# Squared-relu layers: four of the eight scaled copies of x on POOL, the first relu-and-square sooner, the norm's sums one product later

## The reference, cut to what matters

```python
D_FF_2 = 4 * D_MODEL

def sq_relu_mlp(h, w1, w2):
    u = jax.nn.relu(h @ w1)
    return (u * u) @ w2
# in the second block, for l in 0, 1:
#   x = x + mixer(rmsnorm_2(x, norm_mix))
#   x = x + sq_relu_mlp(rmsnorm_2(x, norm_mlp[l]), w1[l], w2[l])
```

## Time and profile before

| | |
|---|---|
| median of 3 runs | 2420.86 us (2419.38 to 2427.39) |
| profiled execution, its own time | 2424.04 us |
| its span | 2422.2 us |
| TensorE busy | 2370.7 us, 98% of the span |
| VectorE, ScalarE, GpSimd busy | 1328.1, 1065.5 and 232.8 us |
| mean granted TensorE clock | 0.994 of full speed |
| chain that ended last | PE 84%, DVE 6%, ACT 5%, issue 3%, DMA 2% |
| the two squared-relu MLPs | from about 1472 and 2058 us of the span |

### The profile page before, as it was taken

The page is one execution under the profiler, slowest core; times in us unless marked ns, Lnnn a source line. Parts: engine busy times, 40 slices in busy tenths (PEclk is TensorE's granted clock), DMA queues, the critical chain, the costliest instruction groups (busy, mean ns, idle before and its releaser), DMA issues.

```text
span 2422.2 us, 30917 instructions
## 1 busy us (share of the span) xinstructions
PE 2370.7 (98%) x12252; PEld 1948.2 (80%) x12252; DVE 1328.1 (55%) x2135; ACT 1065.5 (44%) x1759; POOL 232.8 (10%) x189
## 2 busy tenths in 40 slices
PE   9999999999999999999999999999999899999998
PEld 8888888777777788888887667989987677888987
DVE  5533436688654345433435866735645675763653
ACT  4323224455432334322223456624624785741642
POOL 0100100322102010100100300000000100100100
PEclk9999999999999999999999999999999999999999
DMA  4223223211122132323222214536521112644642
GB/s 153 100 86 104 99 84 105 80 53 53 62 70 72 55 118 70 105 86 114 88 86 88 82 49 131 141 112 157 140 96 61 42 47 64 165 122 120 160 121 70
DMA packets 72865, 230.68 MB, mean 95 GB/s; under 512 B 8081, under 2 KB 16529, under 8 KB 72465
## 3 DMA queue, kind: packets, MB, share of 16 engines
q1 hardware_dynamic: 66096, 205.81, 25.8%
q0 software_dynamic: 6048, 22.02, 5.5%
q10 hardware_dynamic: 576, 0.87, 0.1%
HBM read 226.57 MB, written 2.10 MB: 94 GB/s over the span
## 4 chain that ended last, share of the span: by engine, by line
PE 84%; DVE 6%; ACT 5%; issue 3%; DMA 2%; POOL 0%; POOLq 0%; ACTq 0%; DVEq 0%
PE bank L2158 21%; PE bank L2162 21%; PE bank L2160 21%; PE bank L2176 3%; PE bank L2178 3%; PE bank L2180 3%; PE bank L2342 2%; ACT whi L2463 2%; DMA wraw<-in_stream 2%; PE bank L2304 1%; PE bank L2349 1%; PE bank L2249 1%; PE bank L2245 1%; DVE wlo L2811 1%; PE bank L2247 1%
## 5 line engine op out<-in xcount | busy, mean ns | idle before, releaser
L2811 DVE TENSOR_TENSOR wlo<-wraw,whi 128x1024 fp32r<-128x1024 f32 (+3 forms) x462 | 518.2, 1126 | 556.4 <-ACT whi L2463 555.7
L2463 ACT ACTIVATE whi<-wraw 128x1024 fp32r<-128x1024 f32 (+3 forms) x462 | 435.4, 949 | 469.4 <-PE bank L2162 375.5
L2158 PE MATMUL bank<-hhi,whi 128*128 128x512 f32 x1288 | 514.9, 400 | 2.3 <-ACT hhi L2508 1.0
L2162 PE MATMUL bank<-hhi,wlo 128*128 128x512 f32 x1288 | 504.8, 392 | 1.7 <-DVE wlo L2811 1.6
L2160 PE MATMUL bank<-hlo,whi 128*128 128x512 f32 x1288 | 503.8, 391 | 0.4 <-DVE hlo L2862 0.4
L2158 PEld LDWEIGHTS bank<-hhi,whi 128*128 128x128 f32 x1288 | 242.3, 188 | 57.1 <-issue 7.1
L2162 PEld LDWEIGHTS bank<-hhi,wlo 128*128 128x128 f32 x1288 | 242.1, 188 | 56.0 <-DVE wlo L2811 4.4
L2160 PEld LDWEIGHTS bank<-hlo,whi 128*128 128x128 f32 x1288 | 242.5, 188 | 50.2 <-DVE hlo L2862 2.7
L2160 PE MATMUL bank<-mlo,whi 128*128 128x512 f32 x448 | 176.8, 395 | 0.2 <-DVE mlo L3168 0.2
L2158 PE MATMUL bank<-mhi,whi 128*128 128x512 f32 x448 | 176.9, 395 | 0.0
L2162 PE MATMUL bank<-mhi,wlo 128*128 128x512 f32 x448 | 176.9, 395 | 0.0
(11 more groups left out here) (459 smaller groups left out, 4232.9 us busy)
## 6 DMA issues: line engine op xcount, KB each, us to landing
wraw<-in_stream SPq DMA_DIRECT2D x335, 512.0 KB, 3.5
wraw<-in_stream POOLq DMA_DIRECT2D x34, 512.0 KB, 5.9
wraw<-in_stream SPq DMA_DIRECT2D x32, 192.0 KB, 2.4
wraw<-in_stream SPq DMA_DIRECT2D x22, 256.0 KB, 2.7
rot_tables<-in_stream SPq DMA_DIRECT2D x8, 512.0 KB, 5.2
rot_tables<-in_stream POOLq DMA_DIRECT2D x8, 512.0 KB, 5.4
wraw<-in_stream SPq DMA_DIRECT2D x26, 128.0 KB, 2.0
wraw<-in_stream SPq DMA_DIRECT2D x8, 320.0 KB, 2.9
```

Of the source, the lines that this page charges most:

```text
L2158: pe.matmul(out, sh, xh, start=first, stop=False)
L2162: p = pe.matmul(out, sl, xh, start=False, stop=end and last)
L2463: act.activation(whi[j][:, 0:L], src[:, 0:L], F.Copy).then_inc(*hi.up(c))
L2811: dve.tensor_tensor(wlo[j][:, 0:L], src[:, 0:L], whi[j][:, 0:L].bitcast(f32), SUB).then_inc(*lo.up(c))
```

## The change

Three edits, the same in both MLPs. The scaled copies for feature tiles 0 to 3 go from ACT (an activation with a scale) to POOL (a multiplication by the gain); those for tiles 4 to 7 stay on ACT, and DVE's combination now waits for both. The relu, square and split of plain tile 0 goes ahead of `token_sums(2)`, and `token_sums(3)` goes behind that of plain tile 1. A job that does nothing (`int`) is put between the seven additions and the two `R.step`, so that each of these comes one product later.

```diff
                 ts[0] = run(ts[0])
                 one_more_split()
                 token_sums(1)
+                square(ts[0], 0, afree)
+                one_more_split()
                 token_sums(2)
-                one_more_split()
-                token_sums(3)
                 state["held"] = False
-                square(ts[0], 0, afree)
                 for f in range(1, 4):
                     state["held"] = f == 3
                     square(run(ts[f]), f, afree)
-                owed = chain_of([open_sums[R.next].pay_one] * 7, [R.step] * 2)
+                    if f == 1:
+                        token_sums(3)
+                owed = chain_of([open_sums[R.next].pay_one] * 7, [int], [R.step] * 2)
...
-                elif k == "plain":
+                elif k == "plain" and a[1] >= 4:
                     s, j, q, after = a
                     waits(after)
                     act.activation(tmps[:, q, :], X(s)[:, j, :], F.Copy, scale=gain(s, j)).then_inc(*held.up(("plain", s, j)))
...
                     u1, u2, v1, v2 = tmps[:, u, 0:256], tmps[:, u, 256:512], tmps[:, v, 0:256], tmps[:, v, 256:512]
+                    w.wait_ge(*gated["plain", s, k4])
                     w.wait_ge(*held["plain", s, k4 + 4])
...
+                elif k == "plain" and a[1] < 4:
+                    s, j, q, after = a
+                    waits(after)
+                    w.wait_ge(*before.now())
+                    pool.tensor_scalar(tmps[:, q, :], X(s)[:, j, :], gain(s, j), None, MUL).then_inc(*gated.up(("plain", s, j)))
+                    before = gated
                 elif k == "acc":
                     kind, key, r, plus, settled = a
                     w.wait_ge(*(landed(r) if kind == "low" else added[key] if kind == "row" else lo[settled]))
```

## The result

| | before | after |
|---|---|---|
| median, 6 runs each on the same chip | 2420.72 us (2419.38 to 2427.39) | 2439.04 us (2436.76 to 2443.31) |
| profiled execution, its own time | 2424.04 us | 2438.38 us |
| its span | 2422.2 us | 2436.5 us |
| granted clock | 0.994 | 0.99 |

The ratio on record is 1.007, with a 95% interval of 1.0059 to 1.008; between the two medians lie 18.3 us. The changed kernel is slower. The forecast was 15.7 us slower and 2436.6 us, in a range of 2430.0 to 2442.5 us.

The account below looks back on a forecast made before the run. TensorE, busy 98% of the span, was taken to bound the kernel, so its waits count. 7.76 + 8.21 - 0.3 = 15.7 us on 2420.86 gave 2436.6 us, range 2430 to 2442.5 us.

Parts of the forecast that it names:

- The decisive step: POOL's first copy in each MLP can't begin before its first accumulating DMA is through, at 1487.04 in the first.
- The first sum: DVE's first token sum waits for POOL's first copy, taken as 0.70 us: 8.30 and 8.75 us later.
- TensorE's idle at the third tile: First MLP: TensorE idle from 1484.65 to 1490.83 for `whi3`, third matmul at 1492.1: 7.0 us lost.
- ACT's chain: First sum to the second seven-product chunk's `whi`: 17.6 us, 0.54 less than before; 7.76 and 8.21 us lost per MLP.
- The step from TensorE's 7.0 us to ACT's longer delay: At the third product TensorE waits for ACT again, so the first MLP loses ACT's 7.76 us, not 7.0.
- The norm: Sums one product later: their wait goes, one of 1.63 us at the second MLP's spread comes; together -0.3 us.
- the one on the root: Second MLP's norm: DVE's root stands behind an `mlo` awaiting the `mhi` of 2134.04, beginning at 2135.30 instead of 2132.59.
- The clock: A 1.2 GHz stretch follows the long idle in both MLPs, hidden in lost time: counted nothing, at most 2.5 us each.
- The first, copies in time: Copies run in time and ACT is relieved; head waits of 2.5 and 2 us go: 2416 us, 5%.
- The second, part taken back: ACT's chain isn't the later one, so only TensorE's own loss counts, 4.5 us per MLP: 2430 us, 10%.
- The third, an unhidden low clock: Slow clock outlasts the slack or comes before the seven products, up to 2.5 us per MLP: 2437 to 2442 us, 18%.
- The fourth: The first MLP's slow stretch at the norm goes with the sums' wait and no other comes: 2434 us, 7%.

Follow-up runs that it names:

- the kernel with one copy: The changed kernel with the copies of tiles 1 to 3 back on ACT, only each MLP's first on POOL: 2439.27 us, ratio 1.0065.
- copies alone: The changed kernel with the old order of relus and token sums and without the `int`; POOL's copies stay: 2439.89 us, ratio 1.0074.
- the gap alone: The kernel before with only the norm's sums one product later and its spread two products behind them: 2416.56 us, ratio 0.9979.

## Why the prediction was right, and where its terms were off

**The decisive step held.** The copies stand behind the DMA's wait, the landing is hardly moved by the change, and the copies begin with the wait's end. From the issue at 1478.79 on SP to POOL's DMA at 1484.45 are 5.66 us, and before it was 1480.37 to 1486.03, the same 5.66 us. With the DMA elsewhere the loss is gone, and with the DMA one copy later it is a third.

**The first sum: 8.30 and 8.75 us were forecast, 9.2 us came in both.** Counted from the `wlo` ahead of it, the sum began 1.22 us after that before and 10.44 us after it in after, 9.22 us later (second MLP: 1.23 and 10.38, 9.15 us). The term that was mis-sized is POOL's copy. I took 0.70 us between bounds of 0.53 and 1.29; it took 1.86 us behind the DMA, 1.95 us next, and 1.56 us in the other two places. It is outside my upper bound, too: I had reasoned that one input can't cost more than two. The bound was the fastest of the groups that I could have read. The trace of before has other POOL instructions of 128x512 with two inputs at a mean of 1454 ns (a multiplication, too), 1505 and 1534 ns (sums); with the slowest of them the bound would have been near the 1.56 us of an undisturbed copy:

```profile
L3355 POOL TENSOR_TENSOR qk<-ftmps 128x512 f32<-128x512 f32 x28 | 43.0, 1534 | 2.2
```

The copy's 1.16 us more are partly made up by its beginning 0.78 us after the DMA's start and not 1.01, and, in the second MLP, by a landing that comes 0.5 us sooner after the `wlo` (7.84 us, where it was 8.35). The estimate from the Trainium skill's "GPSIMD Engine Reference", "Elementwise — side-by-side cycle accounting", 0.44 us, was farther off still. By it the sum would have been 0.5 us less (0.26 us twice) and not the 0.3 us that the prediction says.

**TensorE's idle at the third tile:** about 6 us for `whi3` and then its `wlo` were forecast; 7.28 and 6.13 us came, and 0.32 us for the `wlo`. Two labels of the prediction are off without touching a sum: the first MLP has a fifth short wait before the change, 0.53 us for a `wlo` at 1479.55 in the second tile, and it is still there in after; and the waits that I said would remain "at the second and third product" are both the third's.

**ACT's chain: 17.6 us were forecast, 18.44 us came** (1487.13 to 1505.57; before 18.14). My list of gaps came from rows in which POOL was quiet. With POOL copying, three of them are longer: sum to `thi` 1.60 us for 1.19, `whi3` to `wlo` 1.37 us for 1.08, and `wlo` to the third sum 1.53 us for 1.22. That is 1.0 us; the other gaps come to 0.17 us less than my list. So the lighter ACT gave back nothing, where I had put 0.54 us per MLP. Even with the copies in time it is little: in the kernel with the DMA behind them the same chain takes 17.80 us (1482.33 to 1500.13), 0.34 us less than before. That this is POOL beside DVE and not the order is shown by the kernel with one copy, where the same gaps are 1.19, 1.07 and 1.28 us. The step from TensorE's 7.0 us to ACT's longer delay held, as did its sign: at the third product TensorE was late by 9.5 and 9.4 us (7.76 and 8.21 forecast). In the first MLP that is 9.22 + 0.30, the late sum and the chain's 0.30 us over before.

**The norm: -0.3 us were forecast, -2.1 us came** in the kernel with that edit alone. The wait at `ident` was 1.53 and 1.01 us and not 1.63. The step that failed is the one on the root. I had it behind an `mlo` that waits for the `mhi` of 2134.04. But the `mlo` just ahead of the root takes an earlier `mhi`. ACT's and DVE's timelines of after, first MLP, show it: the `mlo` begins before ACT's next `mhi` does.

```profile
1557.01 0.64 ACT L2498 ACTIVATE mhi<-tmps 128x512 fp32r<-128x512 f32 x1
...
1556.77 0.68 DVE L2858 TENSOR_TENSOR mlo<-tmps,mhi 128x512 fp32r<-128x512 f32 x1
1557.37 0.15 DVE L2878 TENSOR_SCALAR sm<-bank 128x4 f32<-128x4 f32 x1
```

The shorter waits are worth some 0.7 us in the two MLPs together (0.1 and 0.6). The rest may be the slow stretch of clock behind the sums ("What the runs showed of the hardware"), which is not shown by medians: the interval is wide enough to hold the forecast's 0.3 us and those 0.7 us alone.

**The clock.** A granted clock of 0.50, which is 1.2 GHz, did follow the long idle in both MLPs, and the matmuls behind it took 0.80 us. It was hidden as argued: TensorE still waited 0.93 and 0.89 us for ACT's `whi` at the third product.

**The rivals.** The first, copies in time, fell with the idle of 9.21 us. Its price was wrong as well: the kernel in which the copies are in time takes 2417.91 us and the norm's edit alone 2418.87, so what the timely copies and the new order add to that edit is within the scatter. The 2.5 and 2 us at the heads went only in small part: the first MLP still has three waits of some 0.8 us in that kernel, 2.44 us in all (the third is 0.76 us, for the `wlo` at 1507.54), and the second has 1.46 us of its 2.06.

```profile
1502.49 0.38 PE L2181 MATMUL bank<-thi,wlo 128*128 128x256 f32 x1 [0.75 <-DVE wlo L2812]
1506.28 0.39 PE L2177 MATMUL bank<-thi,whi 128*128 128x256 f32 x1 [0.93 <-ACT whi L2464]
```

The second, part taken back, would have needed TensorE's own loss to be the later one; ACT's was. The third, an unhidden low clock, didn't happen behind the long idle, though its time of 2437 to 2442 us holds the median: the 9.5 us of each head end before the third product and come from the copy and from DVE. Its other half, a low clock in front of the products, was there at the third product, and for 1.3 us only in the second MLP, where the profiled before has none; the last section shows that it comes and goes with or without the change. The fourth did happen beside the forecast. The first MLP has no slow stretch at its norm in after (clock 1.00 from 1555 to 1560, where it was 0.50 in the earlier trace rows). The stretch that holds it is the one with -3.4 us.

In sum: 18.9 us at the two heads for a forecast of 16.0, and some -2 us at the norms for -0.3, would be 16.8 us; the medians say 18.3, with an interval of about 14 to 19 us. The forecast of the difference was 2.6 us short, and the terms were each off by more than the sum shows, with opposite signs: 2.9 us too little at the heads and 1.8 us too much at the norms. That the time came out so near is in part luck. The median lies 0.5 us above the band of 2435 to 2438.5 us that POOL's bounds gave the forecast, and inside the range.

## What to carry to other kernels

An engine that does nothing isn't free if a wait for a transfer stands in its queue: before giving it work, look at what it sits in and when that ends, and move the wait behind the work. Ask also whether the engine relieved was the late one: here ACT had waited for DVE's sums, so work taken off it bought 0.3 us at best, and the new helper slowed DVE. Where a wait stands ahead of a chain of small dependent steps, the cheap edit is to put other work between the two ends of that chain.

## What the runs showed of the hardware

- A POOL copy of 128x512 with a factor per partition took 1.56 us in most places (all eight of the kernel with the DMA behind the copies are between 1554 and 1569 ns), longer than the fastest group with two such inputs (1286 ns in the earlier trace rows) and about as long as the slowest sum of two (1534 ns). Right behind the issue of a DMA it took 1.85 or 1.86 us in all eight places, also where DVE was idle, and a copy that followed that one, beside DVE's short instructions of the token sum, took 1.95 us in all six.
- While POOL copied, some DVE instructions were longer by 0.36 to 0.41 us: 0.42 became 0.83 us, 0.96 became 1.32, 1.23 became 1.60. In after that is one instruction per POOL copy; others beside the same copy were not longer. In the kernel with the DMA behind the copies, the `tlo` beside the third copy was longer by 0.11 us only (1.07).
- A wait of 1.5 us at the sums, followed by eight matmuls of one column, had a stretch of low clock behind it in some executions and not in others: in 2 of the 6 places with that wait in the profiled executions (before and the two kernels that keep it). Where the sums don't wait, none of 16 places had one. The two with it were in different MLPs and different kernels (0.50 in the earlier trace rows, and the stretch here, copies alone, second MLP). That the wait is what starts it is likely by these counts and not shown; what decides it from one execution to the next stays open. The stretch of the copies alone, clock before the DMA share:

```profile
2145.00:2150.00 5.00, 5.00 (x31) 5.00 (x32) 4.65 (x15) 3.52 (x5) 0.23 (x1) 0.66 0.86 156
```

- The third product shows the same thing more often, and it costs time that the waits don't show. TensorE waits 0.6 to 0.9 us for the `whi`, does two matmuls, and waits 0.76 us for the `wlo`. In 12 of the 20 places with both waits, in ten profiled executions, the clock then went to 0.50, and 22 matmuls took 3.9 to 4.3 us from the second wait's end and not 2.7. In before it is the first MLP alone, with the same waits in both:

```profile
1506.00:1508.00 2.00, 2.00 (x11) 2.00 (x11) 0.37 (x2) 1.33 (x2) 0.15 (x1) 0.50 0.73 74
2091.00:2093.00 2.00, 2.00 (x19) 2.00 (x18) 0.33 (x2) 1.14 (x2) 0.31 (x1) 1.00 0.73 68
```

  So a pair of short waits there is worth 1.6 us, or about 3 when the clock falls. The one place with neither wait, the first MLP of the kernel with the DMA between the first and the second copy, has no low clock. One place is too few, so that the stretch would go with the waits isn't shown.
- In after, TensorE also waits 1.34 us at 2137.13 for a DVE copy out of PSUM, where before the longest such wait there was 0.49 us, at 2122.91. Seven of the nine other kernels have such waits of 0.3 to 1.0 us, 0.82 us in the gap alone, so the copies aren't needed for one. Its cause wasn't followed.
